# Attention stage of a two-layer trunk: projection pieces of six products in steps 8 to 17, a weight split in step 7, first transposes inside a projection unit

## The reference

```python
proj = h @ w_in                     # 1024 -> 3*512 (A: q, k, v) + 512 (B: q) + 128 + 128 (B: k, v)
qa, ka = rope(qa), rope(ka)         # 8 heads of 64, three dilated windows merged
oa = dilated_attention(qa, ka, va)
qb, kb = rope(qb), rope(kb)         # 8 query heads, 2 key/value heads, window 128, sinks
ob, _ = banded_attention(qb, kb, vb, B_WINDOW - 1, sinks)
x = x + concatenate([oa, ob]) @ w_out
```

## Time and profile before

| what | value |
|---|---|
| time, median of 3 runs | 1496.44 us (1495.36 to 1498.22) |
| time of the profiled execution | 1494.55 us |
| its span (first to last instruction) | 1492.4 us |
| PE busy | 1465.2 us, 98% |
| DVE, ACT busy | 1212.0 us, 1013.9 us |
| granted TensorE clock, mean | 0.998 |

### The profile page before, as it was taken

The page is one execution under the profiler, slowest core; times in us unless marked ns, Lnnn a source line. Parts: engine busy times, 40 slices in busy tenths (PEclk is TensorE's granted clock), DMA queues, the critical chain, the costliest instruction groups (busy, mean ns, idle before and its releaser), DMA issues.

```text
span 1492.4 us, 20291 instructions
## 1 busy us (share of the span) xinstructions
PE 1465.2 (98%) x7038; PEld 1216.5 (82%) x7038; DVE 1212.0 (81%) x1474; ACT 1013.9 (68%) x1270; POOL 108.2 (7%) x130
## 2 busy tenths in 40 slices
PE   7999999999999999999999999999999999999997
PEld 6767888888989888888888888888888888888886
DVE  7665654554885679989989989999899999999997
ACT  6556344444523577887887878778788788787775
POOL 0000300000342073000000000000000000001000
PEclk9999999999999999999999999999999999999999
DMA  9414796554633559999999999999999999999993
GB/s 343 166 57 142 277 413 252 195 172 141 198 118 109 169 210 392 408 384 387 388 366 389 395 364 383 399 361 379 395 369 378 391 366 382 387 388 369 390 403 125
DMA packets 198769, 458.96 MB, mean 308 GB/s; under 512 B 8969, under 2 KB 18241, under 8 KB 198721
## 3 DMA queue, kind: packets, MB, share of 16 engines
q1 hardware_dynamic: 190336, 433.12, 79.0%
q0 software_dynamic: 6768, 24.64, 4.2%
q10 hardware_dynamic: 1616, 0.56, 0.2%
HBM read 438.37 MB, written 19.92 MB: 307 GB/s over the span
## 4 chain that ended last, share of the span: by engine, by line
PE 91%; DVE 2%; issue 1%; ACT 0%; DVEq 0%; ACTq 0%
PE bank L1461 28%; PE bank L1463 28%; PE bank L1462 28%; PE bank L1632 2%; PE bank L1761 1%; DVE w_lo L884 1%; PE bank L1477 0%; PE bank L1889 0%; PE bank L1842 0%; PE bank L1790 0%; PE bank L1855 0%; PE bank L1607 0%; PE bank L1599 0%; DVE X L1415 0%; DVE work L1216 0%
## 5 line engine op out<-in xcount | busy, mean ns | idle before, releaser
L884 DVE TENSOR_TENSOR w_lo<-raw,w_hi 128x1024 fp32r<-128x1024 f32 x822 | 971.3, 1228 | 184.8 <-ACT w_hi L546 183.6
L546 ACT ACTIVATE w_hi<-raw 128x1024 fp32r<-128x1024 f32 x822 | 825.5, 1054 | 401.7 <-PE bank L1463 398.6
L1461 PE MATMUL bank<-w_hi,t_hi 128*128 128x512 f32 x1312 | 513.3, 391 | 3.4 <-DVE w_lo L884 1.5
L1463 PE MATMUL bank<-w_hi,t_lo 128*128 128x512 f32 x1312 | 509.1, 388 | 0.0
L1462 PE MATMUL bank<-w_lo,t_hi 128*128 128x512 f32 x1312 | 508.8, 388 | 0.0
L1461 PEld LDWEIGHTS bank<-w_hi,t_hi 128*128 128x128 f32 x1312 | 246.4, 188 | 55.1 <-issue 5.9
L1463 PEld LDWEIGHTS bank<-w_hi,t_lo 128*128 128x128 f32 x1312 | 246.3, 188 | 50.9
L1462 PEld LDWEIGHTS bank<-w_lo,t_hi 128*128 128x128 f32 x1312 | 246.5, 188 | 50.2 <-issue 0.7
L1461 PE MATMUL bank<-w_hi,h_hi 128*128 128x512 f32 x576 | 230.4, 400 | 0.0
L1463 PE MATMUL bank<-w_hi,h_lo 128*128 128x512 f32 x576 | 225.2, 391 | 0.0
L1462 PE MATMUL bank<-w_lo,h_hi 128*128 128x512 f32 x576 | 224.5, 390 | 0.0
(11 more groups left out here) (277 smaller groups left out, 796.3 us busy)
## 6 DMA issues: line engine op xcount, KB each, us to landing
raw<-in_w_gate_moe_dram SPq DMA_DIRECT2D x112, 1024.0 KB, 8.2
raw<-in_w_up_moe_dram SPq DMA_DIRECT2D x112, 1024.0 KB, 9.1
raw<-in_w_down_moe_dram SPq DMA_DIRECT2D x112, 1024.0 KB, 8.0
raw<-in_w_in_rec_dram SPq DMA_DIRECT2D x16, 1024.0 KB, 5.6
raw<-in_w_gate_dense_dram SPq DMA_DIRECT2D x14, 1024.0 KB, 6.0
raw<-in_w_up_dense_dram SPq DMA_DIRECT2D x14, 1024.0 KB, 5.0
raw<-in_w_down_dense_dram SPq DMA_DIRECT2D x14, 1024.0 KB, 4.8
raw<-in_w_in_attn_dram SPq DMA_DIRECT2D x9, 1024.0 KB, 14.6
```

What stands on the lines that cost most here:

```text
L546: act.activation(w_hi[:, (u - 1) % SPL, half], raw[:, r, half], ACT.Copy).then_inc(signal, 1)
L884: dve.tensor_tensor(w_lo[:, s, half], raw[:, r, half], w_hi[:, s, half].bitcast(F32), ALU.subtract).then_inc(signal, 1)
L1461: pe.matmul(o, lh, rh, start=start, stop=False)
L1463: return pe.matmul(o, ll, rh, start=False, stop=stop)
```

## The change

```diff
-FILLER = {0: (6, 0), 1: (6, 1), 2: (7, 0), 3: (7, 1), 4: (8, 0), 5: (8, 1),
-          11: (9, 0), 12: (9, 1), 13: (10, 0), 15: (10, 1)}
-SPLIT_AT = {2: 10, 4: 11, 11: 12, 13: 13}
+FILLER = {0: (6, 0, 0, 4), 1: (6, 1, 0, 4), 2: (7, 0, 0, 4), 3: (7, 1, 0, 4), 4: (8, 0, 0, 4), 5: (8, 1, 0, 4),
+          8: (9, 0, 0, 2), 9: (9, 1, 0, 2), 11: (9, 0, 2, 4), 12: (9, 1, 2, 4),
+          13: (10, 0, 0, 2), 14: (10, 0, 2, 4), 16: (10, 1, 0, 2), 17: (10, 1, 2, 4)}
+SPLIT_AT = {2: 10, 4: 11, 7: 12, 13: 13}
...
                     place(3, 7)
+                    drained(6, 7)
+                    rotate(2 * AH, 2 * AH + BH, 4)
                 if s == 6:
                     saw_product(3)
-                    drained(3, 6, 7)
-                    rotate(2 * AH, 2 * AH + BH + KVH, 4)
+                    drained(3)
+                    rotate(2 * AH + BH, 2 * AH + BH + KVH, 8)
...
             col_unit([4, 5], TT, 0, 2)
+            s = unit()
+            col_half([4, 5], 0, 1, 2, s)
             pe.wait_ge(roped, 2)
             for j in range(4):
                 qk_transposes(j)
-            col_unit([4, 5], TT, 1, 2)
+            col_half([4, 5], 1, 1, 2, s).then_inc(unit_done, 1)
...
                 if s == AH - 1:
-                    pe.wait_ge(roped, 4)
                     for j in range(4, 7):
+                        pe.wait_ge(roped, 4 if j < 6 else 6)
                         qk_transposes(j)
```

More of the change, by code:

```diff
@@ L1495, in col_unit, with col_half @@
                 last.then_inc(unit_done, 1)
-            def col_half(banks, t, h, units, s, n_cols=BLK, mixed=False):
+            def col_half(banks, t, h, units, s, n_cols=BLK, mixed=False, ks=None):
                 per = KC // units
-                for k in range(per):
+                for k in ks or range(per):
                     if k == per // 2:
@@ L1538, in _ @@
                 qk_transposes(j)
-            col_unit([4, 5], TT, 1, 2)
+            col_half([4, 5], 1, 1, 2, s).then_inc(unit_done, 1)
             def filler(s):
-                u, t = FILLER[s]
-                if t == 0:
+                u, t, k0, k1 = FILLER[s]
+                if t == 0 and k0 == 0:
                     slot[0] = unit()
@@ L1561, in filler @@
                     if u == 9 and t == 0:
[L1563 to L1566, removed]
+                        drained(VB[1])
+                    if k0 == 0:
+                        open_bank(OUT_A[u - 9][t])
+                    last = col_half(OUT_A[u - 9], t, 0, 2, slot[0], mixed=True, ks=range(k0, k1))
+                if t == 1 and k1 == 4:
                     last.then_inc(unit_done, 1)
```

## The result

The changed kernel takes 1499.48 us (median of 18 executions, 1497.70 to 1501.32), the kernel before 1496.01 (18 executions beside them, 1494.26 to 1498.41). The ratio is 1.002, 95% interval 1.0014 to 1.0026: slower by about 3 us, between 2.1 and 3.9 (the medians lie 3.5 apart). Forecast was 0.9 us less. The profiled execution took 1497.7 us, with a span of 1496.1 and a mean granted clock of 0.995, before 0.998. Of the 18 executions 17 have a mean clock of 0.994 or 0.995 and one 0.997.

What follows compares the result with a forecast made beforehand. PE, busy 98% of the span, was taken as the bound. First transposes -1.60 and the loop's end +0.66 (3.48 late, 2.82 saved) gave -0.94, so 1496.44 became 1495.5 us, range 1492.8 to 1498.2.

Steps and rivals of the forecast that it cites:

- rival 2: PE's long hole at the scores of head 8 drops the clock; +7 us (1502.5), or 1497.2 if mild; chance 8%.
- the sum: Whole kernel: -1.60 ahead of the loop and +0.66 at its end make -0.94 us, from the median 1495.5.
- The sign that was named for it: Granted clock dipping between 80 and 95 us, named as something that would show the forecast wrong.
- The full +7: Cost if all 8.2 us of PE work from scores of head 8 to head 11 ran at 1.2 GHz.
- First transposes: Start of kernel: 12 matmuls put ahead of PE's 1.60 us wait for DVE's rotation remove it; -1.6 us.
- The rotation: Query part hidden in DVE's idle time in step 4; step 6 becomes 0.72 us shorter, bounds 0 and 0.9.
- The split in step 7: ACT splits unit 12 before its copies, so scores of head 8 come 1.17 us later; PE idles at least 2.1.
- Rival 1: ACT does the split of unit 12 in idle time, costing nothing; 1.9 us earlier, 1493.6; chance 14%.
- The pieces: Six matmuls instead of 12 behind scores in the loop: distance from head 8's to head 9's 2.39 us, not 3.80.
- last steps: End of the loop: pieces in steps 16 and 17 against later waits; taken as 0, bounds -1.2 and +0.8 us.
- Passing on: PE sets the time in the expert stage, so a shift made earlier is carried to the end.
- Rival 3: First wait only moves, as DVE's copies release scores of head 0 late; +0.7 us, 1497.1; chance 6%.

Runs made afterwards that it cites:

- experiment 4: Kernel before with only the split of unit 12 moved to step 7; 1502.23 us, ratio 1.0041.
- experiment 10: Kernel before with only the new table of pieces of six matmuls, split of unit 12 left in step 11; 1495.79 us, ratio 0.9993.
- experiment 11: Kernel before with only the rotation in two parts, query heads in DVE's step 4, key heads in step 6; 1496.71 us, ratio 1.0004.
- experiment 3: Kernel before with only the first transposes of q and k moved into the middle of the second v unit; 1496.0 us, ratio 1.0.
- experiment 5: Kernel before with the first transposes moved, plus 28 small matmuls nobody reads at the start; 1495.94 us, ratio 0.9999.
- experiment 6: Kernel before plus only 28 small matmuls nobody reads at the start; 1498.28 us, ratio 1.0009.
- experiment 12: Kernel before with 7 matmuls nobody reads filling the 1.7 us hole ahead of step 7's transposes; 1496.04 us, ratio 1.0.
- experiment 2: Changed kernel with 11 matmuls nobody reads filling the hole ahead of the scores of head 8; 1496.2 us, ratio 1.0003.

## Why the prediction was wrong

**The step that failed is the clock: rival 2 happened, and the sum had its price at nothing.** The sign that was named for it came, a dip between 80 and 95 us. I gave it 8%, half of it over the bound, on this reasoning: "the waits of 1.7 passed without any fall". That was one execution. The profiles of experiments 4 and 10 show falls at the same 1.71 us hole, those of 10 and 11 falls behind waits of at most 1.0, and of the 31 executions of before beside the last runs five had a mean clock of 0.996 or less (median 1498.2), 14 one of 0.998 (1495.0). The trace of before showed one draw of something that varies, and I took it for a property of the hole. The hole of 2.66 us, with 0.55 us of work and another 0.43 of hole before it, left little room for luck: 17 of 18 executions have a mean clock of 0.995 or less (the one profile shows the place). The rest of the rival held. The place is right, and so is the price per us of work: the lower level lasted 9.4 us (85.76 to 95.1), which by the factor of 1.85 is 5.1 us of work at full clock; at 0.85 each that is 4.3 (measured 4.0), just past the 4.6 us of work from which the rival decides. The forecast of 1495.5 and 4.0 give 1499.5, the measured median, but that is luck: the median of before was 0.4 lower in this series than the 1496.44 that I started from, and the rest of the sum was 0.5 too good (below). The full +7 had 8.2 us of work at the lower level, and the clock came back sooner.

The Trainium skill's rule on this, "TensorE: Matmul & The Clock Gate", section "Loop structure matters more than you think" (matmuls that stand behind a long wait run cold, back-to-back ones don't), speaks for what happened; the trace of after agrees with it in this loop, at 0.50 behind the 2.66 us hole.

**First transposes, -1.6 with bounds -1.4 and -1.6.** Mechanism right, size at the bound: from the first projection matmul to the scores of head 0 it takes 35.01 us now and took 36.44, so -1.43. The copies of DVE (L1004) are next, with 0.32 waited, the 0.17 worked out for the release and a little more. Wrong was to count it in every execution. It is earned only when the start is at full clock; otherwise the removed wait had been covering up to 1.6 us of slow start (experiments 3 to 6 and 12).

**The rotation.** Hidden in step 4 as costed: 0.43 us are idle before the maximum of head 5 where it was 2.42, and it starts 22.55 us behind the scores of head 0, before 22.59. In step 6 the six instructions take from 80.01 to 80.75 us on DVE, 0.74 instead of 1.54: -0.80, forecast -0.72. PE no longer waits for either part.

```profile
71.73 0.29 DVE L1042 CUSTOM_DVE_ANT_0 work<-bank,work 128x128 f32<-128x128 f32 x1 [0.43 <-PE bank L1588]
...
80.01 0.19 DVE L995 TENSOR_TENSOR work<-work,rope 128x32 f32<-128x32 f32 x1 [1.38 <-ACT work L660]
...
80.75 0.28 DVE L1042 CUSTOM_DVE_ANT_0 work<-bank,work 128x128 f32<-128x128 f32 x1
```

**The split in step 7.** Right in each link: exponential, split, copies in this order on ACT, the scores of head 8 0.26 us behind the copies. They come at 85.76; forecast were 86.72 on the time axis of the old trace, less 1.60, plus the start 0.40 later, so 85.52. The hole is 2.66, forecast 2.1 to 2.7. Rival 1 (no hole) is refuted by that.

**The pieces.** At full clock the scores of heads 8 and 9 lie 2.42 us apart (experiment 2), forecast 2.39; in the changed kernel 4.40, by the clock.

**The sum.** Experiment 2 is the world of the forecast, the same order without the fall. Two measured parts make the sum: -1.43 ahead of the loop (after) and +0.97 in it (experiment 2), together -0.46, forecast -0.94. The missing half microsecond is 0.17 of the first term and 0.31 of the loop: the scores of head 11 came 3.64 later (forecast 3.48), and the saved matmuls and last steps gave back 2.67 (forecast 2.82). Experiment 2's executions at full clock, 8 of 12, have a median of 1495.5, which is also the forecast; those of before have 1495.0 to 1495.3, so even with a held clock no gain over before is shown for it. Its profile shows one reason: it started at the lower level, and of the first term only 0.08 was earned in it (36.36 us to the scores of head 0, before 36.44). One slip stands in the range: the upper bounds add up to +0.8, not +0.9.

**Passing on.** Right: the stages behind carry the shift, 907 matmuls in 200 us at clock 1.00. Rival 3 wasn't so.

## What to carry to other kernels

A hole in TensorE's stream has two prices, its length and the clock behind it, and the second can be the larger: here 2.66 us of hole, and 4.0 on the matmuls after it. So work that is needed late (the split of unit 12) must not stand ahead of what TensorE waits for next, and where a hole can't be closed, matmuls that nobody reads can hold the clock in most executions (8 of 12 here). And one profiled execution shows one draw: before a saving of a thousandth is counted on, read the mean clock of many executions, and ask whether the wait that is to be removed was covering a start that varies.

## What the runs showed of the hardware

- The times of a kernel fall into groups by its mean granted clock: before has 1495.0 to 1495.3 at 0.998, 1496.3 to 1496.9 at 0.997, 1498.2 to 1498.5 at 0.996 or less. No fallen execution of before itself was profiled.
- With a hole of 2.66 us 17 of 18 executions have a mean clock of 0.995 or less; with one of 1.50 us 4 of 10 are at 0.996 or less, and with the hole filled 4 of 12. Behind a hole of 1.71 us the clock fell in the profiles of experiments 4 and 10 and held in that of before. It also fell behind waits of at most 1.0 us (experiments 10 and 11, end of the loop).
- The clock rows read the lower level for 10.2 us in the changed kernel, 9.4 of them with PE at work, and for 3.4 us behind the 1.71 us holes of experiments 4 and 10.
- The start costs 0 to 2.9 us by execution at the lower level's matmul durations; the clock row reads 1.00 there in experiment 3 and 0.57 in experiment 10. With 9 small matmuls before the inputs arrive and 5 behind the first transposes the full-clock median went from 1492.9 to 1491.1; 20 and 8 delay the first projection matmul by 1.1 to 2.8 us and cost as much as they save.
